# Encoder layer with routed experts: weight blocks and gate broadcasts issued behind the first gathers

## The reference

```python
def expert_choice_ffn(h, w_router, w_gate, w_up, w_down):
    aff = jax.nn.softmax((hf @ w_router).astype(jnp.float32), axis=-1)
    g, idx = lax.top_k(aff.T, cap)                 # cap 64 (prompt), 128 (sample)
    xe = hf[idx]
    hid = jax.nn.silu(jnp.einsum('ecd,edf->ecf', xe, w_gate)) * jnp.einsum('ecd,edf->ecf', xe, w_up)
    ye = jnp.einsum('ecf,efd->ecd', hid, w_down) * g[..., None].astype(h.dtype)
    y = jnp.zeros((n, D), h.dtype).at[idx.reshape(-1)].add(ye.reshape(-1, D))
...
    x = x + gate2 * expert_choice_ffn(h2, w_router, w_gate, w_up, w_down)
```

## Time and profile before

| | |
|---|---|
| time, median of 3 runs | 3197.74 us (3197.16 to 3198.77) |
| profiled execution: its time | 3197.88 us |
| profiled execution: its span | 3195.8 us |
| mean granted TensorE clock | 0.988 |
| TensorE busy | 97% |
| VectorE busy | 72% |
| ScalarE busy | 60% |
| GpSimd busy | 6% |
| DMA, mean over the span | 217 GB/s |

### The profile page before, as it was taken

One profiled execution on the slowest core, in us unless ns is written; L12 is line 12 of the kernel. 1 busy time (PEld: TensorE's weight loads), 2 busy tenths in 40 slices (PEclk: granted clock), 3 DMA queues, 4 the chain that ended last, 5 costly groups with the idle time before them and its releaser, 6 DMA issues.

```text
span 3195.8 us, 48834 instructions
## 1 busy us (share of the span) xinstructions
PE 3111.8 (97%) x18750; PEld 2789.6 (87%) x18750; DVE 2296.4 (72%) x3531; ACT 1906.4 (60%) x3107; POOL 188.4 (6%) x191
## 2 busy tenths in 40 slices
PE   5999999995999999999999999999999999999998
PEld 4777766785999999999999999999999999999997
DVE  4679938557777777677777777777777777777775
ACT  5154468544666666666666666666666666665664
POOL 0000000001010101010101010010101010101000
PEclk8999999997999999999999999999999999999999
DMA  9421267336675757585757676666757575857562
GB/s 330 138 76 57 60 217 240 134 117 235 234 257 211 267 198 276 195 296 190 286 212 262 231 262 228 247 242 233 257 211 275 199 270 191 296 202 283 214 248 96
DMA packets 143177, 692.73 MB, mean 217 GB/s; under 512 B 11104, under 2 KB 49264, under 8 KB 119664
## 3 DMA queue, kind: packets, MB, share of 16 engines
q1 hardware_dynamic: 133280, 663.55, 55.8%
q0 software_dynamic: 8128, 25.17, 3.1%
q10 hardware_dynamic: 1552, 1.00, 0.1%
HBM read 650.35 MB, written 39.34 MB: 216 GB/s over the span
## 4 chain that ended last, share of the span: by engine, by line
PE 76%; DVE 1%; DMA 0%; issue 0%; ACT 0%; POOL 0%; POOLq 0%; DVEq 0%; ACTq 0%
PE psG L1693 34%; PE psG L1695 16%; PE psY L1712 5%; PE psY L1715 5%; PE psY L1713 5%; PE psY L1714 5%; PE psY L1716 5%; DMA xg<-xhat_d,iall 0%; DVE idxu L1187 0%; DVE affT L1190 0%; DVE vals L1184 0%; ACT xst L1884 0%; POOL out L1758 0%; DVE yp L1960 0%; DVE ye L1954 0%
## 5 line engine op out<-in xcount | busy, mean ns | idle before, releaser
L1693 PE MATMUL psG<-xe,w_gu_hi_part 128*128 128x384 f32 x5632 | 1619.5, 358 | 2.7 <-DVE xe L2022 2.7
L1695 PE MATMUL psG<-xe,w_gu_lo_part 128*128 128x192 f32 x5632 | 1411.4, 251 | 0.0
L1695 PEld LDWEIGHTS psG<-xe,w_gu_lo_part 128*128 128x128 f32 x5632 | 1076.1, 191 | 13.1
L1693 PEld LDWEIGHTS psG<-xe,w_gu_hi_part 128*128 128x128 f32 x5632 | 1058.6, 188 | 16.5 <-DVE xe L2022 3.1
L1935 DVE TENSOR_TENSOR w_gu_lo_part<-raw_gu,w_gu_hi_part 128x1024 fp32r<-128x1024 f32 x704 | 859.7, 1223 | 119.1 <-ACT w_gu_hi_part L1817 119.1
L1817 ACT ACTIVATE w_gu_hi_part<-raw_gu 128x1024 fp32r<-128x1024 f32 x704 | 738.6, 1052 | 14.1 <-DMA raw_gu<-in_w_gu 14.1
L1845 ACT ACTIVATE low<-psG 128x384 f32<-128x384 f32 x352 | 173.0, 491 | 695.0 <-PE psG L1695 694.7
L1970 DVE TENSOR_TENSOR gu<-psG,low 128x384 f32<-128x384 f32 x352 | 196.1, 557 | 495.4 <-ACT low L1845 495.4
L1940 DVE TENSOR_TENSOR w_dn_lo_part<-raw_dn,w_dn_hi_part 128x1024 fp32r<-128x1024 f32 x352 | 431.2, 1225 | 1.0 <-ACT w_dn_hi_part L1828 0.8
L1828 ACT ACTIVATE w_dn_hi_part<-raw_dn 128x1024 fp32r<-128x1024 f32 x352 | 368.1, 1046 | 3.6 <-PE psY L1716 3.6
L1712 PE MATMUL psY<-w_dn_hi_part,hs 128*128 128x512 f32 x704 | 282.6, 401 | 0.0
(11 more groups left out here) (215 smaller groups left out, 3004.6 us busy)
## 6 DMA issues: line engine op xcount, KB each, us to landing
raw_gu<-in_w_gu SPq DMA_DIRECT2D x176, 2048.0 KB, 7.9
raw_dn<-in_w_down SPq DMA_DIRECT2D x176, 1024.0 KB, 8.9
shared<-in_ada_w SPq DMA_DIRECT2D x12, 2048.0 KB, 11.3
w_raw<-in_w_in SPq DMA_DIRECT2D x20, 512.0 KB, 5.4
bias<-in_bias SPq DMA_DIRECT2D x6, 1536.0 KB, 14.7
qk_d<-shared SPq DMA_DIRECT2D x8, 768.0 KB, 3.6
qk<-qk_d SPq DMA_DIRECT2D x8, 768.0 KB, 7.9
out<-x SPq DMA_DIRECT2D x12, 512.0 KB, 2.6
```

Source lines behind the costliest of these rows:

```text
L1693: pe.matmul(bank[:, 0:2 * CAP], wh, xe[:, k, :, :].rearrange("p a b -> p (a b)"), start=(k == 0), stop=False, skip_group_check=True)
L1695: mm = pe.matmul(bank[:, 0:CAP], wl, xe[:, k, 0, :], start=False, stop=(k == KD - 1), skip_group_check=True)
```

## The change

The two broadcasts of `gate2` move from behind `flip` to behind the third block of gate and up and the second block of down. SyncE's wait for the two first gathers moves from the fourth block of gate and up to the third. TensorE's wait at line 1652 is lowered from 48 to 16. VectorE's wait on the same semaphore is not touched. Line numbers from here on in the changed kernel are two higher behind the edit (lines 1623 and 1630, the block loads, are 1621 and 1628).

```diff
--- before.py
+++ after.py
@@ -1609,12 +1609,10 @@
             @block.sync
             def _(sp):
                 sp.dma_start(flip[:, :], A["flip"]).then_inc(gate_loaded, 16)
-                for grp in range(2):
-                    sp.dma_start(gate2[:, grp, :], ada_d[grp:grp + 1, 5 * D:6 * D].to_broadcast([P, D])).then_inc(gate_loaded, 16)
 
                 def load_gu(e, ci, first):
                     back = last_user(ci, RING_GU, CHUNKS)
-                    if first and ci == RING_GU:
+                    if first and ci == RING_GU - 1:
                         sp.wait_ge(g_loaded_p, 16)
                         sp.wait_ge(g_loaded_s, 16)
                     if not (first and back < 0):
@@ -1634,6 +1632,10 @@
                         load_gu(e, ci, first)
                         if ci >= 1:
                             load_dn(e, ci - 1, first)
+                        if first and ci == RING_GU - 1:
+                            for grp in range(2):
+                                sp.dma_start(gate2[:, grp, :], ada_d[grp:grp + 1, 5 * D:6 * D].to_broadcast([P, D])).then_inc(
+                                    gate_loaded, 16)
                     load_dn(e, CHUNKS - 1, first)
                 loads(0, True)
                 with sp.Fori(1, EXPERTS) as e:
@@ -1649,7 +1651,7 @@
                 pe.transpose(psG[:, 1, 0:80], idxf[:, :], ident[0:80, 0:80])
                 pe.transpose(psG[0:CAP_P, 3, EXPERTS:2 * EXPERTS], idxf[0:EXPERTS, own],
                              ident[0:EXPERTS, 0:EXPERTS]).then_inc(tT_done, 1)
-                pe.wait_ge(gate_loaded, 48)
+                pe.wait_ge(gate_loaded, 16)
                 pe.wait_ge(merged, 1)
                 pe.matmul(psG[:, 2, 0:2 * EXPERTS], flip[:, :], top[:, :, 64:80], start=True, stop=True).then_inc(flipped, 1)
```

## The result

| | before | after |
|---|---|---|
| time, median of 5 runs | 3197.74 us (3197.13 to 3198.77) | 3214.37 us (3213.11 to 3215.53) |
| span of the profiled execution | 3195.8 us | 3211.3 us |
| first product starts | 769.88 us | 786.02 us |

The ratio is 1.0051 (95% interval 1.0039 to 1.0062): slower by 16.6 us, where 16.5 was forecast.

The account below looks back on a forecast made before the run. TensorE's first expert product was taken to set the end. Gates in at 773.95 us plus 12.47 put it at 786.4 instead of 769.88, 16.5 later: 3214.3 us on the median, own range 3211 to 3218, 8 in 10 3208 to 3220.

Parts of the forecast that it names:

- What bounds the kernel: TensorE, 97% busy, waits for nothing from the first product on; each microsecond that product shifts moves the end equally.
- The gathers: Large gather ahead of the first product, on an empty queue: lands at about 761.0 instead of 764.5 us.
- What is taken from in front: Broadcasts no longer ahead of the gathers: first down block lands at about 749.5 instead of 754.4 us.
- What is put behind: SyncE's loads after the gathers: 10.4 us to the second down block, 2.5 for the broadcasts; gates in at 773.95.
- the row at 541 us: Two broadcasts behind a long run of loads in the same kernel, 2.5 us; chosen over 4.9 us at 735 us.
- The wait that decides: VectorE, ahead of its first low part, waits for all three loads from 756.2 to 773.95, about 17.8 us.
- The sum behind the wait: From VectorE's passed wait to the first product: 4.93, 0.69, 6.80 and 0.05 us, together 12.47.
- The clock: TensorE's rise from half clock, 5 us after the product began, moves along; a later rise costs 0 to 2 us.
- The range: Forecast's own range, 3211 to 3218 us, from the bounds of gather (-1.8, +3.5), broadcasts (+2.4) and clock (+2).
- overtaking: Rival: broadcasts do not wait for the blocks ahead in SyncE's queue; 3209.4 us, or 3207.0; 7%.
- late gathers: Rival: gather still lands at 764.5 us and broadcasts take 4.9; product 22.4 us later, 3220.1 us; 6%.
- The point at which the wait would decide nothing: VectorE's gate wait passed at 757.4 us at the latest; rival of no binding wait: 3196.5 us, 2%.

Follow-up runs that it names:

- late_wait: The changed kernel with VectorE's wait for both gates moved to the first place that reads a gate, behind expert 0's last down product; 3196.79 us.
- gates_front: The changed kernel with the two broadcasts back behind flip and TensorE's wait back at 48; block 2 and second down block stay behind the gathers; 3195.70 us.
- early_squares: The kernel with late_wait's edit and VectorE's queue reordered ahead of the first product: low parts of tile 0, then yp, then irow; 3195.26 us.
- busy_wait: The changed kernel with 78 added products of the identity with itself on TensorE while it waits for yp; 3213.75 us.
- null_late: The kernel before with VectorE's gate wait moved to the first use of the gates, nothing else; 3197.12 us.
- gates_head: The changed kernel with the two broadcasts issued first behind the wait for the gathers, ahead of block 2 and the second down block; 3207.64 us.
- gates_moved: The kernel before with the broadcasts behind the second down block, SyncE's wait where it was, flip on its own semaphore; 3201.28 us.
- one_more_mb: The changed kernel with the third down block, 1 MB, issued ahead of the two broadcasts instead of behind block 3; 3215.85 us.

## Why the prediction was right

- *What bounds the kernel* held: no wait of TensorE behind the first product in any of the eleven kernels, and the time follows that product.
- *The gathers*: in 4.6 us behind the start (4.5 forecast), by two errors that cancel. The instruction took 0.99 us and not 1.79, and the landing came 3.6 us behind its end and not 2.7. In the kernels with the new order where the instruction took 1.8 us (late_wait, gates_front, early_squares) the landing came 3.3 to 3.4 us behind its end and 5.1 to 5.2 behind its start, 0.6 more than forecast.
- *What is taken from in front*: the first down block in at 735.87 + 14.1 = 750.0 (749.5 forecast).
- *What is put behind*: 10.4 us forecast from the first issue to the down block's landing, 10.2 measured (771.5 - 761.26); 2.5 for the broadcasts behind it, 2.5 measured. The choice of the row at 541 us over that at 735 us was worth 2.4 us and was the nearer one; the exact hit is in part luck, as busy_wait, with the same loads, has 3.4 us there.
- *The wait that decides*: VectorE at 774.10 against 773.95, shown by late_wait and by its idle time. What was wrong in the section on what to look for is the name: the profile says "issue", not the DMA. The gates landed 10.7 and 11.4 us after their issue, where about 12 was given.
- *The sum behind the wait* was 0.5 us too long (11.92 instead of 12.47). The end of `yp` to the product is 6.46 us here and not 6.80, as `ye` had long been copied and its transposes follow 1.74 us behind those of `yp`, not 2.02. The other 0.2 us are the start of `yp`, which comes 0.15 us ahead of the end of `irow`, and the 0.05 counted for waking VectorE.
- *The clock* was given 0 to 2 us of loss and gave 0.6 back: it rose 3.2 us behind the first product instead of 5.4, and the rest of the kernel took 0.64 us less. That the pause did this is not shown: null_late, where TensorE waits 4.8 us for `yp` (4.1 before), has 3.4 as well. Of the hit of 0.1 us on the median, then, some is luck: between the profiled executions the loss is 15.5 us, 1.0 under the forecast, and the runs of the changed kernel scatter by 2.4 us.
- *The range*: the forecast's own range, 3211 to 3218, is said to come from the bounds of its terms, but these add up to 3212.5 to 3222.
- *The rivals*: overtaking is refuted by gates_head and by the landings, which come in the order of issue in the changed kernel, gates_head, gates_moved, one_more_mb and busy_wait; late gathers by the trace. The point at which the wait would decide nothing (the gates in by 757.4) lies between gates_front, which passes it by far, and gates_moved (762.1), which binds.

Not settled: why the instruction of the large gather takes 0.99 us in some kernels and 1.8 in others, and what sets the moment of the clock's rise.

## What to carry to other kernels

Before a load is moved back in a queue, look for every wait that counts it, on every engine, and see where in that engine's queue the wait stands, not where the data is first read; a wait that was met long before it was reached holds up all that is queued behind it once its load is late (17.8 us here, for gates that are first read 165 us after they land). Move the wait to the first reader together with the load. And when an earlier arrival gains nothing, look at what the engine that uses it has queued in front.

## What the runs showed of the hardware that was not expected

At the head of the queue the second of the two broadcasts of one row to 128 partitions lands 2.4 us behind the first or 2.2 us (gates_head, where both are in 5.9 us behind the first one's issue). Behind a stream of block loads both together land 2.5 us behind the last load ahead of them in the changed kernel, one_more_mb and the earlier trace rows, and 3.4 us in busy_wait. Why was not tried.

The moment at which TensorE's clock rises after the first product is not fixed: 3.2 us in the changed kernel, 5.4 in the kernel before, 6.2 in gates_head, behind the same transposes and the same wait of 2.67 us. The windows of the changed kernel:

```profile
788.00:789.00 1.00, 1.00 (x5) 1.00 (x5) 0.00 (x0) 0.00 (x0) 0.93 (x1) 0.50 0.86 299
789.00:790.00 1.00, 1.00 (x7) 1.00 (x7) 0.00 (x0) 0.00 (x0) 0.69 (x2) 0.90 0.35 74
```

In gates_front the clock rose before the product, fell as it began and rose again; in one_more_mb and null_late it was up before the product too, and fell 0.0 and 1.2 us behind its start:

```profile
764.00:766.00 2.00, 0.00 (x0) 0.00 (x0) 1.99 (x6) 1.73 (x3) 1.12 (x2) 1.00 1.06 453
767.00:769.00 2.00, 2.00 (x10) 2.00 (x9) 0.00 (x0) 0.00 (x0) 1.57 (x2) 0.50 1.08 444
770.00:771.00 1.00, 1.00 (x9) 1.00 (x8) 0.00 (x0) 0.00 (x0) 0.70 (x2) 1.00 0.95 393
```

The last two columns of the table go together: with 3.2 to 3.4 us low, the products and all behind them take 2425.3 to 2425.6 us, with 6.2 to 6.3 us 2426.4 to 2426.8. Part of the scatter of the times between executions is of this size.
